# Mixing stage of a hybrid decoder step: pointwise weights multiplied into the lower half of the output weights

## What is computed

```python
glu = u[..., :CONV_WIDTH] * jax.nn.sigmoid(u[..., CONV_WIDTH:])
dw = lax.conv_general_dilated(conv_in, conv_dw[:, None, :], ...) + conv_dw_b
o_conv = jax.nn.silu(layer_norm(dw, conv_ln_g, conv_ln_b)) @ w_pw2
mix = jnp.concatenate([o_attn.reshape(B, T, ATTN_WIDTH), o_conv], axis=-1) @ w_o
x = x + g1 * mix
h2 = rms_norm(x, norm2_g) * (1 + sc2) + sh2
x = x + g2 * (jnp.square(jax.nn.relu(h2 @ w_ff1)) @ w_ff2)
```

## Time and profile before

| | us |
|---|---|
| median of 3 runs | 3267.18 (3265.11 to 3268.1) |
| time of the profiled execution | 3261.57 |
| its span, first to last instruction | 3259.9 |
| mixing stage, first load issued to the last residual add | 1371.5 to 1739.7 |

### The profile page before, as it was taken

How to read it: one execution, slowest core, us unless ns; L and a number is a source line. 1 busy time by engine, 2 the same in 40 slices (tenths; PEclk the granted TensorE clock), 3 DMA queues, 4 the chain that set the end, 5 groups by cost and what they waited for, 6 DMA issues and landing times. The chain is left out here.

```text
span 3259.9 us, 41236 instructions
## 1 busy us (share of the span) xinstructions
PE 2930.0 (90%) x15680; PEld 2407.1 (74%) x15680; DVE 1347.7 (41%) x3391; ACT 912.6 (28%) x2068; POOL 630.8 (19%) x402
## 2 busy tenths in 40 slices
PE   3969996994999976479996999999998999999999
PEld 1238884882777754268884888888887999999998
DVE  1232886995777743355564122111113222222223
ACT  2033331111556542134443111222222122222211
POOL 0000000000000000034432333333332233333331
PEclk8979997996999997679998999999999999999999
DMA  8655433655465227544434211212134231111112
GB/s 285 213 166 194 164 115 112 237 197 152 133 192 169 79 72 291 179 151 130 141 122 132 92 57 46 97 52 97 46 110 124 92 103 46 46 46 46 46 46 107
DMA packets 282389, 401.36 MB, mean 123 GB/s; under 512 B 29792, under 2 KB 221564, under 8 KB 275636
## 3 DMA queue, kind: packets, MB, share of 16 engines
q1 hardware_dynamic: 257484, 297.93, 28.2%
q0 software_dynamic: 3632, 75.50, 6.5%
q10 hardware_dynamic: 21078, 25.30, 2.3%
HBM read 315.10 MB, written 150.99 MB: 143 GB/s over the span
## 5 line engine op out<-in xcount | busy, mean ns | idle before, releaser
L2174 PE MATMUL ff_u_ps<-ff_h_hi,ff_w_hi 128*128 128x352 f32 (+1 forms) x1280 | 452.6, 354 | 18.4 <-DVE ff_h_lo L2092 16.8
L2175 PE MATMUL ff_u_ps<-ff_h_lo,ff_w_hi 128*128 128x352 f32 (+1 forms) x1280 | 450.6, 352 | 0.0
L2176 PE MATMUL ff_u_ps<-ff_h_hi,ff_w_lo 128*128 128x352 f32 (+1 forms) x1280 | 450.0, 352 | 0.0
L2174 PE MATMUL ff_u_ps<-ff_a_hi,ff_w_hi 128*128 128x352 f32 (+1 forms) x1280 | 448.8, 351 | 0.0
L2175 PE MATMUL ff_u_ps<-ff_a_lo,ff_w_hi 128*128 128x352 f32 (+1 forms) x1280 | 448.3, 350 | 0.0
L2176 PE MATMUL ff_u_ps<-ff_a_hi,ff_w_lo 128*128 128x352 f32 (+1 forms) x1280 | 447.9, 350 | 0.0
L2022 POOL TENSOR_TENSOR ff_w_lo<-ff_w_raw,ff_w_hi 128x1024 fp32r<-128x1024 f32 x128 | 307.1, 2399 | 569.8 <-ACT ff_w_hi L2047 569.8
L2132 DVE TENSOR_TENSOR ff_sqr<-ff_relu 128x352 f32<-128x352 f32 (+1 forms) x160 | 98.6, 617 | 642.3 <-ACT ff_relu L2075 642.3
L2115 DVE SCALAR_TENSOR_TENSOR ff_y<-ff_u_ps,modT,ff_y 128x512 f32<-128x512 f32 (+2 forms) x280 | 178.7, 643 | 432.6 <-PE ff_u_ps L2176 432.6
L2047 ACT ACTIVATE ff_w_hi<-ff_w_raw 128x1024 fp32r<-128x1024 f32 x128 | 134.7, 1052 | 626.5 <-PE ff_u_ps L2176 605.8
L2174 PEld LDWEIGHTS ff_u_ps<-ff_h_hi,ff_w_hi 128*128 128x128 f32 x1280 | 241.9, 189 | 44.0 <-POOL ff_w_lo L2022 17.3
(11 more groups left out here) (245 smaller groups left out, 4793.4 us busy)
## 6 DMA issues: line engine op xcount, KB each, us to landing
ff_w_raw<-in_w_ff_dram SPq DMA_DIRECT2D x128, 512.0 KB, 3.9
out_new_k_sample_dram<-in_cache_k_dram POOLq DMA_DIRECT2D x8, 4088.0 KB, 15.2
out_new_v_sample_dram<-in_cache_v_dram POOLq DMA_DIRECT2D x8, 4088.0 KB, 15.8
w_ring<-in_w_ada_dram SPq DMA_DIRECT2D x12, 2048.0 KB, 10.9
sa_kn<-in_cache_k_dram SPq DMA_DIRECT2D x16, 1024.0 KB, 16.0
sa_vn<-in_cache_v_dram SPq DMA_DIRECT2D x16, 1024.0 KB, 18.7
mx_acc<-acc_d SPq DMA_DIRECT2D x16, 768.0 KB, 9.0
x_st<-in_x_prompt_dram ACTq DMA_DIRECT2D x16, 512.0 KB, 6.4
```

The source lines that it names most:

```text
L2174: pe.matmul(out, w_hi[:, b, w], hi, start=first, stop=False)
L2175: pe.matmul(out, w_hi[:, b, w], lo, start=False, stop=False)
L2176: return pe.matmul(out, w_lo[:, b, w], hi, start=False, stop=last)
```

## The change

The product w_pw2 @ w_o[512:1024] is computed once, ahead of tile 0, and takes the place of the lower half of w_o; the swished convolution is then the lower half of the mixed vector.

- `pointwise`, c_ps, y_hi, y_lo, wp_hi and wp_lo go. y_a is split straight into m_hi[4:8] and m_lo[4:8].
- New on TensorE: w_pw2 (wp_raw) is turned by 16 transposes, copied by ScalarE (wpT), and eight groups of four plain fp32 matmuls (128x128 by 128x512) go round three PSUM banks (f_ps and the two z_ps). ScalarE takes the hi part out of each group (wo_hi), VectorE the lo part (wo_lo).
- The loads are ordered anew: w_pw2 in one piece of 1 MB, the lower half of w_o in one of 2 MB, statistics, acc, x, and then the upper half of w_o in four pieces through w_raw.
- Queues: TensorE's turn_o(i+1) stands ahead of project(i,1) (it stood behind it). ScalarE's split_mix(i+1) stands ahead of swish(i+1). VectorE's update is issued in two halves, split_mix(i+1) between the first of them and gate_y. TensorE waits for update half by half.

```diff
-            c_ps = ps("c_ps", [P, CC, P])
+            f_ps = ps("f_ps", [P, 512])
...
+            fold_ps = [f_ps, z_ps[0], z_ps[1]]
...
                     load_conv(0)
-                    for n in range(WN):
+                    sp.dma_start(wp_raw[:], I["w_pw2"][0].rearrange("(k p) c -> p k c", p=P)).then_inc(S["wp_in"], 16)
+                    sp.dma_start(wl_raw[:], I["w_o"][0, AW:D, :].rearrange("(k p) c -> p k c", p=P)).then_inc(S["wl_in"], 16)
+                    for a in range(3):
+                        sp.dma_start(stat[:, :, a].rearrange("p i s h -> p i (s h)"),
+                                     st_d[a].rearrange("(i p) c -> p i c", p=P)).then_inc(S["stat_in"], 16)
+                    load_rest(0)
+                    load_conv(1)
+                    for n in range(WU):
                         if n >= 2:
                             sp.wait_ge(S["w_lod"], n - 1)
...
+                    for j in range(CC):
+                        act.wait_ge(S["wt_pe"], j + 1)
+                        act.activation(wpT[:, j], fold_ps[j % 3][:], ACT.Copy).then_inc(S["wt_d"], 1)
+                    split_w(0)
+                    split_w(1)
+                    swish(0)
+                    act.wait_ge(S["fac_e"], 1)
+                    act.activation(fac[:], fac[:], ACT.Exp).then_inc(S["fac_x"], 1)
+                    for g in range(NF):
+                        m, cols = fold(g)
+                        act.wait_ge(S["wf_pe"], g + 1)
+                        act.activation(wo_hi[:, WU + m, cols], fold_ps[g % 3][:], ACT.Copy).then_inc(S["wf_hi"], 1)
+                        if g in (1, 3):
+                            split_w(2 + g // 2)
+                    split_mix(0)
                     for i in range(NT + 1):
                         if i < NT:
+                            split_mix(i + 1)
                             swish(i + 1)
-                            split_mix(i + 1, 0)
                         if 1 <= i:
                             modulate(i - 1)
-                        if i < NT:
-                            split_mix(i + 1, 1)
                         square(i)
...
+                    for g in range(NF):
+                        m, cols = fold(g)
+                        v.wait_ge(S["wf_hi"], g + 1)
+                        v.tensor_tensor(wo_lo[:, WU + m, cols], fold_ps[g % 3][:], wo_hi[:, WU + m, cols].bitcast(F32), ALU.subtract).then_inc(S["wf_lo"], 1)
+                        if g in (1, 3):
+                            split_w(2 + g // 2)
                     split_mix(0)
...
+                        update(i, 0)
                         if i < NT:
+                            split_mix(i + 1)
                             gate_y(i + 1)
                             split_y(i + 1)
-                        update(i)
-                        if i < NT:
-                            split_mix(i + 1)
+                        update(i, 1)
...
                     turn_dw(0)
+                    pe.wait_ge(S["wp_in"], 16)
+                    for j in range(CC):
+                        if j == 3:
+                            pe.wait_ge(S["wt_d"], 1)
+                        for k in range(CC):
+                            mm = pe.transpose(fold_ps[j % 3][:, k * P:(k + 1) * P], wp_raw[:, k, j * P:(j + 1) * P], ident[:])
+                        mm.then_inc(S["wt_pe"], 1)
                     turn_y(0)
+                    pe.wait_ge(S["wl_in"], 16)
+                    pe.wait_ge(S["wt_d"], CC)
+                    for g in range(NF):
+                        m, cols = fold(g)
+                        if g >= 3:
+                            pe.wait_ge(S["wf_lo"], g - 2)
+                        for j in range(CC):
+                            mm = pe.matmul(fold_ps[g % 3][:], wpT[:, j, m * P:(m + 1) * P], wl_raw[:, j, cols], start=j == 0, stop=j == CC - 1)
+                        mm.then_inc(S["wf_pe"], 1)
                     turn_o(0)
-                    pointwise(0)
+                    pe.wait_ge(S["wf_lo"], NF)
                     for i in range(NT + 1):
                         if i < NT:
                             turn_dw(i + 1)
                         project(i, 0)
                         if i < NT:
                             turn_y(i + 1)
+                            turn_o(i + 1)
                         project(i, 1)
-                        if i < NT:
-                            turn_o(i + 1)
                         if i >= 1:
                             turn_x(i - 1)
-                        if i < NT:
-                            pointwise(i + 1)
```

## The result

The changed kernel takes 3279.99 us (median of 4 runs, 3277.99 to 3282.59), the kernel before, run beside it, 3266.14 us (3261.65 to 3268.1). The ratio is 1.0045, with a 95% interval from 1.0027 to 1.0062: slower by 14 us. The forecast was 3265.8 and no change.

The account below looks back on a forecast made before the run. TensorE was taken as the bound, then a loop through y_n with period 18.75 us against 18.93: 14.6 us less in the tiles, 13.2 lost ahead, -1.4 in all, so 3265.8 us; range 3243 to 3286.

Parts of the forecast that it names:

- rival C: Ahead of tile 0: the clock doesn't rise during the fold's second part, 42.4 us instead of 23.3, 3285 us; chance 0.17.
- the main account: Whole kernel: period 18.75 us, tile 0 late by 13.2, total 3265.8 us, own range 3254 to 3278; chance 0.60.
- a loop over y_n: Mixing stage: layer_norm's y_n is late beside GpSimd's residual and merge; turn_y waits, TensorE idles 3.8 us per tile.
- R: Mixing stage: time zero of the forecast's period, the start of tile i's residual add on GpSimd; next R at 17.25 us.
- the last two residuals: End of the mixing stage: R(15) comes 13.4 us after its forerunner and R(16), without pointwise, 12.1 us.
- Rival A: Mixing stage: the clock holds through 3.8 us of idle, VectorE's 17.4 us is the period, 3246.9 us; chance 0.17.
- Rival B: Mixing stage: small VectorE operations don't wait for GpSimd, period 16.0 us, 3227 us; chance 0.06.
- The start of y_n: layer_norm in the mixing stage: small operations wait to R+8.8, so y_n begins at R+8.87 and ends at R+9.7.
- The price of the clock: TensorE in the mixing stage: slow restart after idle costs 2.0 us in three periods of four, 1.5 on the mean.
- The bound of 2.14: Upper bound of a restart's cost, from tile 0's first projection half: 7.84 us against 5.70.
- the sum: Mixing stage: 14 periods of 18.75 us plus the last two, 14.6 us less, with 13.2 lost ahead: -1.4 us.
- Ahead of tile 0: Fold before the first tile: 0.53 us per 512-column record and late evictions make the first residual 13.2 us later, bounds 9 to 17.

Follow-up runs that it names:

- f2: Changed kernel with the store of x1 issued by ScalarE behind the square, not by GpSimd ahead of the merge: 3267.62 us, ratio 1.0009 to the kernel before.
- e3: Changed kernel with 16 more matmuls of 128x512 per tile ahead of turn_y, their result unused: 3256.61 us, ratio 0.9978 to the kernel before.
- e2: Changed kernel with the nine two-tensor operations of each reciprocal root in the mixing stage taking a per-partition scalar instead: 3233.25 us, ratio 0.9902 to the kernel before.
- f3: Changed kernel with the fold's evictions ahead of tile 0 put before the w_o splits and softmax factors: 3268.73 us, ratio 1.0016 to the kernel before.
- e4: Changed kernel with the old queue orders and the one-input small operations together: 3188.34 us, ratio 0.9766 to the kernel before.
- f4: Changed kernel with old queue orders, one-input small operations and earlier fold evictions together: 3178.73 us, ratio 0.9735 to the kernel before.
- h2: As h1, but GpSimd's merge waits until second_norm's small operations are done (rs2_d in place of yn_d): 3229.41 us, ratio 0.9894 to the kernel before.
- h1: e1 with one wait more: GpSimd begins a tile's merge only when VectorE has written its y_n: 3225.88 us, ratio 0.9889 to the kernel before.
- e1: Changed kernel with the old queue orders on TensorE, ScalarE and VectorE, the fold kept: 3272.13 us, ratio 1.0023 to the kernel before.

## Why the prediction was wrong, step by step

The measured 3280 lies in the stated range, 3243 to 3286, but only because rival C, which didn't happen, had widened it upwards; the main account ended at 3278. That is luck. (The range's "6 to 8 us" for the period are 6.3 and 9.1 by its own ends, 14 x 0.45 and 14 x 0.65.)

Right were these: that TensorE's bound would go and a loop over y_n would take its place; the wait of TensorE (3.8 us of idle forecast for TensorE, 4.6 measured); that one-element operations with two tensors wait for GpSimd, and where those waits end (forecast R+2.4, R+6.1, R+7.45, R+8.8; measured R+2.40, R+6.10, R+7.44, R+8.78); that the clock falls in that idle time; the last two residuals (13.4 and 12.1 us forecast, 13.36 and 11.93 measured). Rival A (the clock holds) and rival B (no waits) are out by the 0.50 in the stretch above and by the 3.28 us. Rival C is out too: the clock rose in the fold's second part (its first eight records took 5.54 us, the next eight 3.4 to 3.6).

Wrong were three terms, two of which weigh.

1. **The start of y_n.** The step read "they wait to ... R+8.8. So y_n begins at R+8.87": as if the last waiting operation were the last of layer_norm. It was the sixth of the nine. One round of the iteration is still to be done behind it: four small operations and a gap, 1580.38 to 1581.42, 1.04 us. y_n began at R+9.82. This makes 0.95 us a period. GpSimd's four operations stopped four of the nine, here and in f2; I should have laid out all nine in time instead of only the ends of the waits.

2. **The price of the clock.** The step took 2.0 us "in three periods of four, 1.5 on the mean". It was 2.4 us in every one of the 14: the eight transposes of y and o took 1.62 us up to the first matmul of the half (0.84 forecast), and from there the residual came 8.29 us later instead of 6.67. e3, without it, has 18.10 instead of 20.49. The bound of 2.14 came from a row in which only a half of the projection ran slowly; here the transposes ahead of it did too. Part of the price hangs on term 1. f2 has the idle time that was forecast, 3.8 us instead of 4.6, and there the granted clock was 0.83 in only four periods of 14 and 0.91 in the other ten. An estimate from TensorE's busy time in one period, 13.6 us at full clock in e2 and 15.1 and 16.4 us in f2's short and long periods, gives some 1.5 and 2.7 us there, some 1.8 on the mean. So a mean over tiles was not wrong in kind; but no period went free, and the idle time was longer than forecast. The Trainium skill ("TensorE: Matmul & The Clock Gate", HAM oscillation — how this bites in real kernels) tells of a loop whose wait slows the clock in every round, so that each one starts slow; the trace of after agrees, in each of the 14 periods at 20.5 us.

The two together give 17.25 + 0.95 + 2.40 = 20.6, as measured (20.49 on the mean). Against the 18.75 of the sum that is 14 x 1.74 = 24.4 us.

3. **Ahead of tile 0.** 13.2 us were forecast, 10.2 came (the first residual 73.3 us after the first load of the stage, 63.1 before). A record of a fold matmul took 0.43 us at full clock (3.43 us from one group of eight to the next) and not 0.53. The two ends of the range stood in the text, and the row for 512 columns was the nearer one; I had added to it a weight load that isn't exposed. The cause of the loss was named rightly (the evictions stand behind the loads in the queues), and f3 gives its price: 9.5 us of the kernel's time.

The sum again: -1.4 + 24.4 - 3.0 - 0.2 = +19.8 us for the stage; 19.7 were measured. Terms 1 and 2 alone turn "no change" into "slower".

There is also a judgement behind terms 1 and 2. The forecast's own range for the period was 18.3 to 19.4 us, and its slower side was given to rival C, a mishap ahead of tile 0. The bound of the clock was written down as 2.14 us and the idle time as 3.8; with the upper bound alone the period would have been 19.4 and the time 3275. And where every unknown of a loop has its cheap end in the sum, the dear ends are a rival of their own.

## What to carry to other kernels

When the bounding engine gets shorter, lay out the whole period of the next chain operation by operation, with what the neighbours do at the same time. Here a chain of tiny VectorE operations came to lie beside GpSimd's merge, and GpSimd's 5.3 us entered the critical path. The removal of 5.3 us of matmuls gave 14 us of loss as it was and a gain of 76 and 86 us with two and three small edits elsewhere (e4, f4): a change should be judged only when its new bound has been looked at. Idle time of TensorE that recurs in each round is to be priced at its length plus a slow restart in every round: 2.4 us behind 4.6 us of idle here, an estimated 1.5 or 2.7 behind 3.8 us in f2.

## What the hardware showed that I had not expected

- A VectorE operation on 128x1 elements took up to 3.28 us beside a GpSimd operation. It is stopped if it reads two tensors from SBUF; written with a per-partition scalar (0.21 us) it isn't (e2). Operations that aren't tiny are stopped too (h2: 3.31 us for 0.75, 1.77 for 0.69), and GpSimd by them in turn (1.61 for 1.30). The Trainium skill ("SBUF — State Buffer", SBUF: two separate sides) describes a pair of ports that the two engines share, taken for the whole of an instruction by whichever began first. The Trainium skill ("GPSIMD Engine Reference", Key points) names VectorE's operations with two SBUF inputs and its two-port modes as those that contend. The 3.31 us of h2 agree with a lock for the whole instruction: both records begin at 1551.41, GpSimd's takes its 2.76 us, and x1n ends 0.55 us behind it. The 3.28 us agree in where they end, but not in who came first: that record begins 0.47 us ahead of the merge's.
- GpSimd's DMA issue of 0.59 us doesn't stop these operations: 45 of them begun beside one take 0.15 or 0.16 us each (h1). It costs by its place: with it gone from between residual and merge, y_n comes 0.82 us earlier (f2).
- The same idle time of TensorE, 3.8 us, has two prices in one kernel (f2): in ten periods the granted clock is 0.91 and the period 18.73 to 19.25 us, in four it is 0.83 and the period 20.11 to 20.22.
- 256 more matmuls of 512 columns in the stage made the changed kernel 22 us faster (e3): TensorE idles 0.7 us a tile instead of 4.6, and the clock stays up.
- A wait added to GpSimd made the kernel 44 us faster (h1 against e1).

Left open: in e1, e2 and f2 the periods of one kernel come in two lengths, and the granted clock goes with them. In e1 it is 0.91 in the periods of 18.86 to 19.15 us and 0.83 in those of 20.20 to 20.54; in e2 it is 1.00 at 15.96 and 0.90 at 17.35 to 17.53; in f2 0.91 and 0.83. So there the steps are the clock's; what makes it stay low for longer in one tile than in the next wasn't tried. In h2 they aren't: one period of 17.47 us has a clock of 1.00, and one of 17.45 has the 0.95 of one of 16.28. What makes those long isn't known.
